# Twelve modulation blocks in rows of 1024 columns, the mLSTM values by seven products, later blocks one projection later

## What is computed

```
mod = silu(c) @ ada_w + ada_b                 # 2048 -> 6 x 2048
sh1, sc1, g1, sh2, sc2, g2 = split(mod)
h = rms(x) * (1 + sc1) + sh1
z = h @ w_in                                  # 16 projections of 512 columns, 20 small columns
y = concat(mlstm(m_*), moba(b_*), retention(r_*), nsa(n_*)) @ w_out
x = x + g1 * y
h2 = rms(x) * (1 + sc2) + sh2
out = x + g2 * moe(h2)                        # 32 experts, 4 groups, top 1 group, top 2 in it
```

## Time and profile before

| | us |
|---|---|
| timed runs, median (lowest, highest) | 1635.54 (1634.64, 1638.21) |
| profiled execution, span | 1640.1 |
| its own time beyond the span | not given by the page |
| TensorE busy | 1370.1 (84%) |
| TensorE weight loads | 803.5 (49%) |
| VectorE busy | 650.7 (40%) |
| ScalarE busy | 194.9 (12%) |
| GpSimd busy | 30.5 (2%) |
| moved by DMA | 611.94 MB, mean 373 GB/s |

### The profile page before, as it was taken

How to read it: one execution, slowest core, us unless ns; L and a number is a source line. 1 busy time by engine, 2 the same in 40 slices (tenths; PEclk the granted TensorE clock), 3 DMA queues, 4 the chain that set the end, 5 groups by cost and what they waited for, 6 DMA issues and landing times.

```text
span 1640.1 us, 18412 instructions
## 1 busy us (share of the span) xinstructions
PE 1370.1 (84%) x7629; PEld 803.5 (49%) x7629; DVE 650.7 (40%) x968; ACT 194.9 (12%) x482; POOL 30.5 (2%) x35
## 2 busy tenths in 40 slices
PE   5999999999999999998777677677678677767767
PEld 4668888678888758863323123123123123213223
DVE  4557783799873568432221120120121121212213
ACT  2002212211122011130100100100001001001001
POOL 0000100000000000010000000000000000000000
PEclk9999999999999999999888888798787788888888
DMA  9997787667866776989999999999999999999996
GB/s 397 427 427 291 295 335 300 256 269 283 336 250 250 281 275 278 380 356 381 430 428 428 428 428 428 428 428 428 428 428 428 428 429 428 428 428 429 428 428 291
DMA packets 44539, 611.94 MB, mean 373 GB/s; under 512 B 4896, under 2 KB 5168, under 8 KB 6736
## 3 DMA queue, kind: packets, MB, share of 16 engines
q1 hardware_dynamic: 42848, 604.00, 88.6%
q0 software_dynamic: 1072, 6.44, 0.9%
q10 hardware_dynamic: 576, 0.89, 0.2%
HBM read 609.21 MB, written 2.10 MB: 373 GB/s over the span
## 4 chain that ended last, share of the span: by engine, by line
DMA 50%; PE 44%; DVE 5%; issue 1%; SPq 0%; ACT 0%; DVEq 0%
DMA ring<-in_exp_w 34%; PE W L714 14%; DMA Zpad<-in_exp_w 9%; PE W L691 7%; DMA ring<-in_stream 5%; PE M L1150 5%; DMA tail<-in_exp_w 3%; DVE tail L1513 2%; PE A L1168 2%; PE W L1031 2%; PE W L665 2%; PE W L1058 2%; PE W L699 2%; PE W L1102 1%; PE M L675 1%; PE W L1115 1%
## 5 line engine op out<-in xcount | busy, mean ns | idle before, releaser
L1150 PE MATMUL M<-ring,g1b 128*32 128x512 f32 x1280 | 183.9, 706 | 76.8 <-DMA ring<-in_exp_w 76.6
L1513 DVE SCALAR_TENSOR_TENSOR tail<-ring,small,tail 128x512 f32<-128x512 f32 x300 | 225.6, 752 | 10.5
L1446 DVE TENSOR_TENSOR consts<-A,tail 32x512 f32<-32x512 f32 x128 | 87.9, 686 | 162.0 <-PE A L1168 159.0
L1150 PEld LDWEIGHTS M<-ring,g1b 128*32 128x32 f32 x1280 | 38.9, 120 | 186.9 <-DMA ring<-in_exp_w 113.3
L2051 DVE SCALAR_TENSOR_TENSOR tail<-tail,M 128x128 f32<-128x128 f32 x32 | 9.2, 288 | 298.8 <-ACT tail L1423 298.8
L1168 PE MATMUL A<-Zpad,tail 128*32 128x512 f32 x512 | 88.1, 820 | 31.5 <-DMA Zpad<-in_exp_w 24.2
L691 PE MATMUL W<-buf_h,ring 128*128 128x256 f32 x512 | 111.9, 379 | 0.0
L1122 PEld LDWEIGHTS M<-consts,tail 128*128 128x128 f32 x512 | 65.7, 201 | 93.0 <-ACT tail L1425 60.3
L714 PE MATMUL W<-ring,buf_x 128*128 128x256 f32 x480 | 108.7, 384 | 2.3 <-DVE ring L1446 2.3
L691 PEld LDWEIGHTS W<-buf_h,ring 128*128 128x128 f32 x512 | 96.7, 190 | 12.9
L714 PEld LDWEIGHTS W<-ring,buf_x 128*128 128x128 f32 x480 | 91.8, 192 | 15.5 <-DVE ring L1446 2.5
(11 more groups left out here) (333 smaller groups left out, 1371.9 us busy)
## 6 DMA issues: line engine op xcount, KB each, us to landing
ring<-in_exp_w SPq DMA_DIRECT2D x96, 2048.0 KB, 36.7
ring<-in_stream SPq DMA_DIRECT2D x88, 2048.0 KB, 12.2
Zpad<-in_exp_w SPq DMA_DIRECT2D x56, 2048.0 KB, 38.0
PPY<-in_exp_w SPq DMA_DIRECT2D x24, 2048.0 KB, 30.7
tail<-in_exp_w SPq DMA_DIRECT2D x16, 2048.0 KB, 45.2
Zpad<-in_early SPq DMA_DIRECT2D x8, 1536.0 KB, 10.6
buf_x<-in_x SPq DMA_DIRECT2D x2, 1024.0 KB, 6.9
buf_h<-in_x POOLq DMA_DIRECT2D x1, 2048.0 KB, 12.2
```

What stands on the lines that cost most here:

```text
L1150: ins = pe.matmul(M[32 * j:32 * j + 32, 512 * w13:512 * w13 + 512], XT[:, kk, 32 * q:32 * q + 32], w[:, 512 * k:512 * k + 512], start=(kk ...
L1446: return dve.tensor_tensor(o, x, y, op)
L1513: ins = dve.scalar_tensor_tensor(acc, w, cs[:, kk:kk + 1], acc, ALU.mult, ALU.add)
```

## The change

It does four things.
- `is_wide` names the blocks 8 to 15 and 20 to 23. Two neighbouring wide blocks (an even number and the next) now share a range of 1024 columns: the even one holds rows 0 to 1023 of it, the odd one rows 1024 to 2047, and a half holds four tiles of 128x1024. `ada_rows` does four instructions on 1024 columns for a half instead of eight on 512, into the same place of `g2b`. `ADA_LATER` is reordered so that neighbours are adjacent columns, and the host lays the stream out to match. Blocks 16 to 19 stay as they were.
- m_v is done by seven products. Its sums come behind block 12 and ahead of the convolution of m_k on VectorE; its separate weight sum goes to `g1b`.
- Because of that GpSimd's load of the g1 bias moves to the step `sums_24` of m_o, behind m_v's fifth product. ScalarE's wait before it writes m_v's place moves from the step `chunk` to `sums_24` of m_v.
- Blocks 13 to 19 move one projection later: 13 behind m_o, 14 behind b_v, 15 behind r_v, 16 behind b_q, 17 behind b_k, 18 behind r_q, 19 and 20 both behind r_k. The stream follows. By `place_sums` the sums move too: `ada_rows` 1 comes behind b_q's products, `ada_turn` 1 and the sum of block 16 come one behind the other after b_k's, the sums of 17, 18 and 19 after those of r_q, r_k and r_g.

```diff
--- before.py
+++ after.py
@@ -58,7 +58,7 @@
 
 
 N_PAIRED = 8
-ADA_LATER = [16, 12, 17, 13, 18, 14, 19, 15, 8, 9, 10, 11, 20, 21, 22, 23]
+ADA_LATER = [16, 17, 12, 13, 18, 19, 14, 15, 8, 9, 10, 11, 20, 21, 22, 23]
 N_ADA = N_PAIRED + len(ADA_LATER)
 
 ADA_BEHIND = {1: N_ADA - 2, 2: N_ADA - 1}
@@ -70,7 +70,7 @@
 EARLY = ('n_kc', 'n_vc', 'n_q')
 EARLY_CORNERS = {'n_ks': 3, 'm_o': 2}
 FIRST_PRODUCTS = {'b_k': 4}
-SEVEN = ('n_ks', 'n_vs', 'n_kw', 'n_vw', 'm_o', 'b_v', 'r_v', 'b_q', 'b_k')
+SEVEN = ('n_ks', 'n_vs', 'n_kw', 'n_vw', 'm_v', 'm_o', 'b_v', 'r_v', 'b_q', 'b_k')
 ALL_SEVEN = SEVEN + ('out1', 'out2')
 ORDER = [('extras', 0), ('sums_31', 'n_ks'), ('sums_24', 'n_ks'), ('blocks', 0), ('gates', 0),
          ('chunk', 'n_ks'), ('sums_31', 'n_vs'), ('cmp_hid', 0), ('sums_24', 'n_vs'), ('norm', 'n_q'),
@@ -79,16 +79,17 @@
          ('chunk', 'n_kw'), ('ada', 9), ('cmp_kT', 0), ('sums_31', 'n_vw'), ('sums_24', 'n_vw'), ('cmp_scores', 0),
          ('chunk', 'n_vw'), ('turn', 'n_ks'), ('ada', 10), ('corners', 'n_vw'), ('norm', 'n_kw'), ('cmp_pT', 0),
          ('chunk', 'm_q'), ('ada', 11), ('cmp_pv', 0), ('scores', 'slc'), ('conv', 'm_q'),
-         ('chunk', 'm_k'), ('turn', 'n_kw'), ('ada', 12), ('turn_p', 'slc'), ('conv', 'm_k'),
-         ('chunk', 'm_v'), ('ada', 13), ('pv', 'slc'), ('sums_31', 'm_o'), ('sums_24', 'm_o'), ('scores', 'win'),
-         ('chunk', 'm_o'), ('ada', 14), ('sums_31', 'b_v'), ('turn_p', 'win'), ('sums_24', 'b_v'), ('pv', 'win'),
-         ('chunk', 'b_v'), ('ada', 15), ('sums_31', 'r_v'), ('m_decay', 0), ('sums_24', 'r_v'), ('turn_y', 'n'),
-         ('chunk', 'r_v'), ('ada', 16), ('sums_31', 'b_q'), ('m_scores', 0), ('sums_24', 'b_q'),
-         ('chunk', 'b_q'), ('ada', 17), ('sums_31', 'b_k'), ('m_pv', 0), ('sums_24', 'b_k'), ('norm', 'b_q'),
+         ('chunk', 'm_k'), ('turn', 'n_kw'), ('ada', 12), ('sums_31', 'm_v'), ('turn_p', 'slc'), ('sums_24', 'm_v'),
+         ('conv', 'm_k'),
+         ('chunk', 'm_v'), ('pv', 'slc'), ('sums_31', 'm_o'), ('sums_24', 'm_o'), ('scores', 'win'),
+         ('chunk', 'm_o'), ('ada', 13), ('sums_31', 'b_v'), ('turn_p', 'win'), ('sums_24', 'b_v'), ('pv', 'win'),
+         ('chunk', 'b_v'), ('ada', 14), ('sums_31', 'r_v'), ('m_decay', 0), ('sums_24', 'r_v'), ('turn_y', 'n'),
+         ('chunk', 'r_v'), ('ada', 15), ('sums_31', 'b_q'), ('m_scores', 0), ('sums_24', 'b_q'),
+         ('chunk', 'b_q'), ('ada', 16), ('sums_31', 'b_k'), ('m_pv', 0), ('sums_24', 'b_k'), ('norm', 'b_q'),
          ('m_out', 0), ('early', 'b_k'), ('turn', 'b_q'),
-         ('chunk', 'b_k'), ('ada', 18), ('corners', 'b_k'), ('turn_y', 'm'), ('norm', 'b_k'), ('turn', 'b_k'),
-         ('chunk', 'r_q'), ('scores', 'moba'), ('ada', 19), ('turn_p', 'moba'),
-         ('chunk', 'r_k'), ('pv', 'moba'), ('ada', 20), ('r_scores', 0),
+         ('chunk', 'b_k'), ('ada', 17), ('corners', 'b_k'), ('turn_y', 'm'), ('norm', 'b_k'), ('turn', 'b_k'),
+         ('chunk', 'r_q'), ('scores', 'moba'), ('ada', 18), ('turn_p', 'moba'),
+         ('chunk', 'r_k'), ('pv', 'moba'), ('ada', 19), ('ada', 20), ('r_scores', 0),
          ('chunk', 'r_g'), ('r_pv', 0), ('turn_y', 'b'), ('turn_y', 'r'), ('ada', 21)]
 
 BETWEEN_HALVES = (('gates', 0), ('turn', 'n_q'), ('cmp_scores', 0), ('cmp_pT', 0), ('scores', 'slc'), ('turn_p', 'slc'),
@@ -144,6 +145,11 @@
 NORMS = [a for s, a in ORDER if s == 'norm']
 MIXED = 'nmbr'
 MIX_Y = {'m': 0, 'n': 1, 'b': 2, 'r': 3}
+
+
+def is_wide(n):
+
+    return N_PAIRED <= n < N_TURNED or n >= N_SUMMED
 
 
 def part_of(n):
@@ -397,7 +403,7 @@
 
             if name[:3] == 'out':
                 return consts[:, N_FIRST + 1024:N_EARLY], tmp[:, 1024:2048]
-            return g1b[:] if name[0] == 'n' else pad[:, 0:2048]
+            return g1b[:] if name[0] == 'n' or name == 'm_v' else pad[:, 0:2048]
 
         def sums_before(name):
 
@@ -564,8 +570,8 @@
                     pool.tensor_scalar(rst, ss, 1.0 / DH, EPS, ALU.mult, ALU.add).then_inc(sem["norm_mean"], 1)
                     pool.wait_ge(sem["norm_mean"], NORMS.index(arg) + 1)
                     rsqrt(rst).then_inc(sem["norm_rstd"], 1)
-                elif (step, arg) == ('corners', 'n_vw'):
-                    pool.wait_ge(sem["products_done"], products_before('n_vw') + 4)
+                elif (step, arg) == ('sums_24', 'm_o'):
+                    pool.wait_ge(sem["products_done"], products_before('m_v') + 4)
                     pool.wait_ge(sem["late_loaded"], 16)
                     pool.dma_start(g1b[:], a['ada_b'][0:1, 2 * D:3 * D].to_broadcast([P, D])).then_inc(
                         sem["late_loaded"], 16)
@@ -1236,7 +1242,9 @@
 
             for step, arg in ORDER:
                 if step == 'sums_24':
-                    if arg == 'm_o':
+                    if arg == 'm_v':
+                        act.wait_ge(sem["turned"], 1)
+                    elif arg == 'm_o':
                         act.wait_ge(sem["turned"], 2)
                     elif arg == 'b_v':
                         act.wait_ge(sem["o_done"], 1)
@@ -1274,9 +1282,7 @@
                     item_done(act, 'chunk', arg)
                     act.wait_ge(sem["chunk_copied"], chunk_no(arg) - 1)
 
-                    if arg == 'm_v':
-                        act.wait_ge(sem["turned"], 1)
-                    elif arg == 'r_q':
+                    if arg == 'r_q':
                         act.wait_ge(sem["scores_done"], 2)
                     elif arg == 'r_k':
                         act.wait_ge(sem["m_pv_done"], 1)
@@ -1496,22 +1502,22 @@
 
                 i = STREAM.index(('ada', n, hf))
                 dve.wait_ge(slot_full[i % RING], 16 * (i // RING + 1))
-                acc = ada_s[n % 2][:]
-                if N_PAIRED <= n < N_TURNED:
-                    acc = g2b[:, 512 * (n % 4):512 * (n % 4) + 512]
-                if n >= N_SUMMED:
-                    c = n - N_SUMMED
-                    acc = g2b[:, 512 * c:512 * c + 512]
-                    if hf == 0:
-                        dve.wait_ge(sem["late_loaded"], 48)
-                for k in range(8):
-                    w = ring[i % RING][:, 512 * k:512 * k + 512]
-                    kk = 16 + 8 * hf + k
+                if is_wide(n):
+                    tiles, width, first = 4, 1024, 16 + 8 * (n % 2) + 4 * hf
+                    acc = g2b[:, 1024 * (n // 2 % 2):1024 * (n // 2 % 2) + 1024]
+                else:
+                    tiles, width, first = 8, 512, 16 + 8 * hf
+                    acc = ada_s[n % 2][:]
+                if n >= N_SUMMED and hf == 0:
+                    dve.wait_ge(sem["late_loaded"], 48)
+                for k in range(tiles):
+                    w = ring[i % RING][:, width * k:width * k + width]
+                    kk = first + k
                     if kk == 16 and n < N_SUMMED:
                         ins = dve.tensor_scalar(acc, w, cs[:, kk:kk + 1], None, ALU.mult)
                     else:
                         ins = dve.scalar_tensor_tensor(acc, w, cs[:, kk:kk + 1], acc, ALU.mult, ALU.add)
-                    if k < 7:
+                    if k < tiles - 1:
                         ins.then_inc(sem["dve_step"], 1)
                         dve.wait_ge(sem["dve_step"], step_no())
                 ins.then_inc(sem["ada_half_used"], 1)
@@ -2099,6 +2105,10 @@
         w = np.asarray(inputs['ada_w'][0, rows])
         return rows_by_partition(np.concatenate([w[:, D + 256 * arg:D + 256 * arg + 256],
                                                  w[:, 256 * arg:256 * arg + 256]], 1), 8)
+    if kind == 'ada' and is_wide(arg):
+        first = 1024 * (arg % 2) + 512 * hf
+        o = 512 * ADA_LATER[(arg - N_PAIRED) // 2 * 2]
+        return rows_by_partition(inputs['ada_w'][0, first:first + 512, o:o + 1024], 4)
     if kind == 'ada':
         o = 512 * ADA_LATER[arg - N_PAIRED]
         return rows_by_partition(inputs['ada_w'][0, rows, o:o + 512], 8)
```

## The result

| | before | after |
|---|---|---|
| timed runs, median (lowest, highest) | 1635.09 (1631.14, 1638.21), 4 runs | 1661.08 (1655.88, 1663.41), 4 runs |
| profiled execution, span | 1640.1 | 1659.4 |
| its own time | not given by the page | 1661.21 |
| TensorE busy | 1370.1 | 1371.9 |
| VectorE busy | 650.7 | 640.2 |

The ratio is 1.0141, 95% interval 1.0118 to 1.0163: slower by 19.3 to 26.7 us. The quotient of the two medians, 1.0159 or 26.0 us, lies inside this interval, above its middle. "Its own time" is the device time of the execution that was profiled, 1.8 us more than its span. The direction and the mechanism were forecast, the size was not: 1653.1 was predicted, and 1661.08 lies above the range's end of 1658.0.

A forecast was written before the change was run, and what follows sets the result against it. TensorE's work plus its waits was taken to bound the kernel up to some 720 us, then the experts' weights. 6.9 + 7.4 + 6.0 - 2.7 = +17.6 us on the median 1635.54 gave 1653.1, range 1643 to 1658.

The forecast's parts named there:

- corner's wait, and clock: At m_v's fifth product, which needs the corner ScalarE copies: a wait of 1.4 us and 1.5 of clock.
- m_o's wait: At m_o's sums from VectorE: a wait of 0.9 us in place of 2.3, without clock loss, a gain of 3.2.
- 2. wait behind b_k, and clock: Sum of block 16 after b_k waits for VectorE, busy with block 17: 5.6 us and 1.8 of clock, +7.4.
- Step 1: m_v by seven products: third product waits 8.7 us for VectorE's sums behind block 12; +6.9 up to m_o's end.
- Step 3: r_g's first half waits for r_k's second half's slot; landing 7.5 us, wait 4.2 and 1.8 of clock, +6.0.
- Step 5: Changes held to cost nothing: block 12's earlier release, the moved bias loads, ScalarE's extra corners, equal bytes.
- Step 4: Output projection: wide block 22 lets the last loads go 1.0 us earlier; the wait falls to 0.9, -2.7.
- Each wait costs twice: After a TensorE wait the matmuls run at a lower clock: 1.8 us lost after 2.32, 1.7 after 1.91.
- (b): One later wait, at b_k's turn or r_g's load, is smaller or absent: 1645.7 to 1647.1 us; chance 0.2.
- (c): Only the m_v part counts, both later waits absent: +4.2, 1639.7 us; chance 0.05.
- (e): VectorE runs ahead, both VectorE waits vanish and only 6.0 at r_g is lost: 1631.4 us; chance 0.05.
- (d): Wide multiply-adds at 1.57 add 1.8 at m_v, short waits each lose 1.7 of clock: 1656 to 1660; chance 0.06.

The follow-up runs named there:

- the one with the tiny products: The kernel before with 12 tiny 32 by 32 products ahead of the turning of x: 1636.63 us, ratio to before 1.0007.
- the narrow blocks: The changed kernel with every modulation block 512 wide again, blocks still in the moved places: 1659.55 us, ratio to before 1.0137.
- the reordered kernel: The changed kernel with m_v's sums before block 12, four steps behind b_k before block 17, r_g's first half loaded before block 20: 1636.08 us.
- the last version: The changed kernel with three reorderings (m_v's sums, steps behind b_k, r_g's load), m_v's corner copied two heads earlier and 16 tiny products: 1631.62 us.
- the fetch moved: The changed kernel with 16 tiny 32 by 32 products ahead of the turning of x, shifting the instruction fetches: 1653.74 us, ratio to before 1.0106.
- r_g early: The changed kernel with r_g's first half loaded ahead of block 20's two halves: 1654.28 us, ratio to before 1.0119.
- the turn ahead: The changed kernel with VectorE's reading of the turned sums (`ada_turn` 1) ahead of block 17: 1659.01 us, ratio to before 1.0136.

## Why the prediction was right or wrong

**What held.** "A microsecond won or lost before 710 us moves the end by one": the routing moved by 20.6 us, the span by 19.3.

| step | forecast | measured in the trace |
|---|---|---|
| 1. wait at m_v's third product | 8.7 | 8.52 |
| clock behind it | 1.8 | 2.3 (9.39 - 7.07) |
| corner's wait, and clock | 1.4 + 1.5 | 0.54 + 0 |
| m_o's wait | 0.9, no clock | 0.97, no clock |
| up to the end of m_o | +6.9 | +5.3 (374.00 to 379.30) |
| clock at r_v, without a wait | none | 1.7 (8.86 against 7.17) |
| 2. wait behind b_k, and clock | 5.6 + 1.8 | 5.54 + 2.2 |
| 3. wait at r_g, and clock | 4.2 + 1.8 | 4.43 + 1.6 |
| 4. output projection | -2.7 | -0.5 |
| at routing | +17.6 | +20.6 |
| length behind the routing | 0 | -1.3 (927.6 to 926.3) |

The clock behind b_k is (2.04 - 1.02) + (1.91 - 1.04) + (14.43 - 14.08) = 2.2, against the same groups at full clock; the start of the output projection is 21.06 us late, and the routing 20.6, which gives the -0.5. Step 1's wait is confirmed by two edits: with the sums ahead of block 12 it is gone, with block 12 narrow it is 10.83. The rows behind it held: 1.316 us for a wide multiply-add against 1.33 by the starts of plain ones. The corner's wait was small since its copy came some 0.4 us earlier than in the sum, and TensorE arrived 0.5 us later, because the clock cost 2.3 us there and not the 1.8 that the sum took; and the 0.54 us that were left cost no clock, where I had charged 1.5. Step 3's landing was 7.8 us where I took 7.5. Step 5 showed nothing that costs.

The Trainium skill's formula for an fp32 tensor_tensor ("VectorE: DVE Perf Modes"), 1.22 us at 1024, is met by the plain ones (1.22 to 1.23) and not by the wide multiply-adds, which pass at 1.316. Its fit for a DMA ("DMA: Bandwidth & Descriptors", the anatomy of one DMA), which it gives for the software queue, makes 6.8 us of 2 MB; no load on SyncE's queue met that, the shortest in any trace here is 7.4.

**Step 4 failed: "The 1.91 us wait falls to 0.9 ... so its 1.7 of clock goes too: -2.7".** The wide block is 1.0 us shorter there (5.25 us for the four instructions of its first half, 6.25 for eight narrow ones), and with the blocks alone widened, the wait is 0.98 and the clock is kept, as in the sum. In the changed kernel the load for the second half landed in 8.8 us instead of 7.8; VectorE's wait for it grew to 5.44 us, its sums came 1.2 us late for TensorE (a new wait), and it began block 22's second half at 674.81, 22.1 us behind before's 652.69 while TensorE was 21.1 behind: the microsecond saved was spent. The last load then took 1.2 us longer from that release (693.93 - 674.81 - 5.26 = 13.9, against 671.65 - 652.69 - 6.29 = 12.7), with a further fetch in it. The two waits together grew by 1.2 (from 0.1 and 1.91), the clock gave back 1.7. That the late landing is the cause is shown (with it gone, the waits are under 0.2 and 0.83); that the fetch makes it late rests on thirteen traces, one edit among them, and another edit speaks against the simple form of it. My bounds for the step, 0 to -3.6, held -0.5, but I took a value beyond their middle from one row, and forgot that two transfers lie in between.

**The clock.** "Each wait costs twice" was right for the three long waits in both traces of the changed kernel, at 1.6 to 2.6 us. It was wrong as a fixed price for short ones. A wait of 2.3 and one of 1.9 us cost 1.7 each in two traces of before and nothing in the one with the tiny products; the changed kernel's 2.06 cost nothing; and at r_v 1.7 are lost with no wait, behind twelve records on four partitions (407.56 to 409.73), in five of the fourteen traces: after, its repeat, the narrow blocks, the reordered kernel and the last version. The Trainium skill ("TensorE: Matmul & The Clock Gate", the part on the HAM clock gate) says of a kernel's start that the number of matmuls done at the low clock differs from run to run of the same kernel; in the middle of this one the three traces of before's order show the like, with 1.7, 1.7 and 0 us lost behind the same wait.

**From the trace to the median: "They lie lower, so I add the difference to the median".** This step failed as well, and it is the largest of the errors and the one that took the number out of its range. My difference was 17.6 and the spans differ by 19.3, an error of 1.7. The medians differ by 26.0. The profiled execution of after has 1.8 us outside its span; with as much, that of before stands at 1641.9, 6 us above the median and above each of its four timed runs; of the 80 different times on record for this kernel (median 1635.5), seven reach it. That of after (1661.21) is at its median. So my sum subtracted, from a typical execution, gains that only a slow one had to give: 1.8 of clock at m_o and 1.7 at the last load. The trace of before with the tiny products shows such an execution: the same waits, no clock loss, routing at 708.93 instead of 712.53, own time 1634.8. Without these 3.5 us the sum is 21.1 and the forecast 1656.6; with r_v's 1.7 it is 1658.3, past the range's end.

Told against this trace, the steps of the sum read otherwise. Up to the end of m_o it is +7.3 for 6.9: the 1.8 of clock that was not there to win and the 0.5 more lost at m_v nearly cancel with the corner, which cost 2.4 less than forecast. That was luck. Then come 1.7 at r_v, 7.7 and 6.0 as before, and +1.1 at the output projection, where -2.7 was forecast. That makes 24.2 us at the routing and, with 2.2 behind it (926.3 against 924.1), 26.4 in all, where the medians are 26.0 apart. One trace is not proof of what is typical. How often an execution of before loses the clock is not known from three traces; the ratio's interval, 19.3 to 26.7 us, takes in the difference of the traces at its lower end.

**The rivals.** (b), (c) and (e) are out: all three of the long waits stood. (d) came nearest in time (1656 to 1660), for the wrong reason, since the wide form is as quick as forecast. My own range for the forecast, 1649 to 1658, counted waits and landings; it left no room for where the profiled execution stood among the runs.

## What to carry to other kernels

When a queue is a fixed list, moving a producer's work into an idle place costs what stands behind it: write down the list of the engine, with starts and ends, and look at whom the moved piece now stands in front of (block 12 before the sums, 17 before the turn and the corners, 20 before r_g). The same instructions in another order were 25 us apart. Removing one such wait shows the next one behind it, so trace the whole list before pricing a fix. And before a loss seen in one profiled execution is booked as a gain, ask whether the median pays it: compare the profiled execution's own time with the timed runs, and keep gains that are clock losses out of the forecast when it lies above them.

## What the runs showed of the hardware

- Half clock after an idle TensorE is not a function of the wait: 2.31 us cost 1.7 in two traces and 0 in a third, of the same work; behind the waits of 4.2 to 10.8 us it cost between 1.5 (r_g with the fetch moved, 15.41 against 13.90) and 3.2 (m_v with r_g early, 10.22 against 7.07).
- The clock can fall without any wait, behind small products on 4 partitions: 8.86 us for 7.17 us of work, granted clock 0.79 around it. It does so in five of the fourteen traces.
- A 16 KB instruction fetch 5.1 to 5.3 us behind the issue of a 2 MB load goes with a landing of 8.7 to 9.0 us instead of 7.6 to 7.9, in seven traces against six; one fetch 6.9 us behind goes with 7.9. Here adding instructions at the start of the program moved such fetches, and with them two waits by 2.4 us together.
- The stretch behind the routing, whose work is the same in all kernels, took 920.3 to 928.3 us in the fourteen traces. Part of this is the clock in its first 40 us: it is 0.87 in the traces of before, of after and of after's repeat, the three longest stretches (926.3 to 928.3), 0.91 in the repeat of before and in the kernel with the turn ahead (924.4 and 924.7), and 1.00 in the other nine (920.3 to 924.3). The waits there are the same in all of them (1.37 to 1.39, 0.30 to 0.33, 0.72 and 0.56 us). What sets the rest is not known, and differences of that size between two single traces are not to be read as effects of an edit.
